# First projection from unnormalised x, the row factor in the activation's scale, and an output projection fed block by block

## The reference

```python
def rmsnorm(x, g):
    xf = x.astype(jnp.float32)
    y = xf * lax.rsqrt(jnp.mean(xf * xf, axis=-1, keepdims=True) + EPS)
    return (y * g.astype(jnp.float32)).astype(x.dtype)

def gmlp_mixer(h, w_in, v_norm_g, w_s, b_s, w_out):
    z = jax.nn.gelu(h @ w_in)
    u, v = jnp.split(z, 2, axis=-1)
    v = rmsnorm(v, v_norm_g)
    w = jnp.where(mask[None], w_s, 0)
    v = v.reshape(B, S // GMLP_BLOCK, GMLP_BLOCK, GMLP_GROUPS, GMLP_GROUP_DIM)
    s = jnp.einsum('gij,bnjgc->bnigc', w, v) + b_s.T[None, None, :, :, None]
    out = u * s.reshape(B, S, GMLP_WIDTH)
    return out @ w_out
...
    h = x
    for l in range(DEPTH):
        if l < N_A_LAYERS:
            h = h + gmlp_mixer(rmsnorm(h, a_norm_g[l]), a_w_in[l], a_v_norm_g[l],
                               a_w_s[l], a_b_s[l], a_w_out[l])
...
        h = h + conv_ffn(rmsnorm(h, f_norm_g[l]), f_w_in[l], f_conv_w[l],
                         f_conv_b[l], f_w_down[l])
```

## Time and profile before

| | us |
|---|---|
| median of 3 runs | 2847.23 |
| lowest and highest | 2845.84, 2847.35 |
| time of the profiled execution | 2847.23 |
| its span in the trace | 2845.2 |
| PE busy in the span | 2670.1 |
| DVE, ACT, POOL busy | 856.2, 565.5, 442.2 |

### The profile page before, as it was taken

The page is one execution under the profiler, slowest core; times in us unless marked ns, Lnnn a source line. Parts: engine busy times, 40 slices in busy tenths (PEclk is TensorE's granted clock), DMA queues, the critical chain, the costliest instruction groups (busy, mean ns, idle before and its releaser), DMA issues. The chain is left out here.

```text
span 2845.2 us, 27418 instructions
## 1 busy us (share of the span) xinstructions
PE 2670.1 (94%) x9989; PEld 1402.6 (49%) x9989; DVE 856.2 (30%) x1933; ACT 565.5 (20%) x1072; POOL 442.2 (16%) x390
## 2 busy tenths in 40 slices
PE   6999999999999999999999989999989999999992
PEld 5644444444656444444444447666745544444440
DVE  2023222102323232221022335556533323222225
ACT  1211111111333211110025542122111111111111
POOL 3004555510000100000121001101110111111110
PEclk8999999999999999999989999999988999999996
DMA  8214555522212222223222110000042699999985
GB/s 172 74 60 133 147 147 147 164 75 57 60 46 60 72 74 74 74 74 84 79 82 74 40 49 25 25 30 16 23 156 89 259 418 416 405 398 400 389 343 213
DMA packets 290831, 407.24 MB, mean 143 GB/s; under 512 B 14258, under 2 KB 253560, under 8 KB 264608
## 3 DMA queue, kind: packets, MB, share of 16 engines
q1 hardware_dynamic: 274048, 366.46, 37.2%
q0 software_dynamic: 16112, 37.19, 4.4%
q10 hardware_dynamic: 560, 2.10, 0.2%
HBM read 396.20 MB, written 30.46 MB: 150 GB/s over the span
## 5 line engine op out<-in xcount | busy, mean ns | idle before, releaser
L925 PE MATMUL bank<-hT,bring 128*128 128x512 f32 x1344 | 582.1, 593 | 0.0
L925 PEld LDWEIGHTS bank<-hT,bring 128*128 128x128 f32 x1344 | 253.8, 190 | 311.9 <-issue 311.9
L864 PE MATMUL bank<-bring 128*128 128x512 f32 x704 | 303.3, 593 | 0.0
L1534 PE MATMUL bank<-bring 128*64 128x512 f32 (+1 forms) x512 | 227.0, 596 | 2.5 <-issue 1.6
L864 PEld LDWEIGHTS bank<-bring 128*128 128x128 f32 x704 | 133.5, 190 | 166.5 <-issue 166.5
L1985 DVE SCALAR_TENSOR_TENSOR ffw<-bank,col,ffw 128x511 f32<-128x511 f32 x88 | 65.9, 749 | 415.0 <-ACT ffw L1633 414.8
L1633 ACT ACTIVATE ffw<-bank,col 128x512 f32<-128x512 f32 x88 | 68.4, 777 | 492.8 <-PE bank L925 470.1
L1970 DVE TENSOR_TENSOR xT<-bank,xT 128x512 f32<-128x512 f32 x32 | 22.1, 691 | 378.2 <-PE bank L864 378.2
L1534 PEld LDWEIGHTS bank<-bring 128*64 128x64 f32 (+1 forms) x512 | 77.8, 157 | 97.7 <-issue 96.5
L663 POOL TENSOR_TENSOR ysq<-ysq 128x512 f32<-128x512 f32 x24 | 30.4, 1268 | 606.7 <-ACT ysq L1605 605.9
L1110 PE MATMUL bank<-hT,bring 128*128 128x512 f32 x256 | 118.7, 611 | 3.6 <-DVE ysq L2142 3.6
(11 more groups left out here) (458 smaller groups left out, 3659.9 us busy)
## 6 DMA issues: line engine op xcount, KB each, us to landing
bring<-f_w_in SPq DMA_DIRECT2D x88, 512.0 KB, 5.3
bring<-exp_w_gate SPq DMA_DIRECT2D x32, 1024.0 KB, 11.0
bring<-exp_w_up SPq DMA_DIRECT2D x32, 1024.0 KB, 19.5
bring<-exp_w_down SPq DMA_DIRECT2D x32, 1024.0 KB, 22.0
two<-ada_w SPq DMA_DIRECT2D x24, 1024.0 KB, 5.3
bring<-f_w_down SPq DMA_DIRECT2D x16, 1408.0 KB, 7.1
two<-exp_w_gate SPq DMA_DIRECT2D x16, 1024.0 KB, 10.1
two<-exp_w_up SPq DMA_DIRECT2D x16, 1024.0 KB, 20.5
```

The costliest lines, as they stand in the source:

```text
L864: mm = pe.matmul(ps[BANKS[stage][n % 4]][:], w[:, k, n % per * P:(n % per + 1) * P], rhs[:, k, :], start=(k == 0), stop=(k == kb - 1))
L925: mm = pe.matmul(ps[2 * j + b][:], w[:, k, b * P:(b + 1) * P], hT[:, k, :], start=(k == 0), stop=(k == KB - 1))
L1534: mm = pe.matmul(ps[3][m * h:m * h + m, :].rearrange("p (m n) -> p m n", m=2), hgT[par][:, k, m * h:m * h + m], w, start=(k == 0), stop=(k ...
```

## The change

- SP issues x, ten rows of gains (tile 0 of `prow`), and then the ring loads. The other 19 parameter rows are issued by ACT, ahead of its first work.
- POOL issues its seven loads behind the constants, and `relR` is the second count of `col_ready`.
- DVE writes `yT`, x times the gain and not normalised, straight from the transposed banks, and gv is computed from `yT`. ACT sums the squares of each token's row from the untransposed x, and the inverse root `row_inv` goes into the takes of gv as the activation's scale.
- `hT`, which gu needs, is made by DVE after unit 0 of gv: PE spreads `row_inv` over 128 partitions into bank 7 by four small products, and DVE multiplies by them. `relR` and the clearing of `wsraw` come behind that on DVE.
- The transposes of the other parameter rows and of `wsraw` move between units 0 and 1 of gu, and the Silu of `c` behind gu.
- go uses banks 4 to 7 and runs its first four output blocks together, k by k. The product of k and n waits only for gated block max(k, n).
- Several semaphores are merged or renamed, and counts of later norms are lowered by one, since the first norm no longer takes part in them.

```diff
--- before.py
+++ after.py
@@ SP: what is left of the parameter loads
-            sp.wait_ge(s("pool_order"), 2)
             for r, ap in ((C_A, a["a_norm_g"][0]), (C_KV, a["kv_norm_g"]), (C_B, a["b_norm_g"][0]),
...
-                row_load(0, r, ap)
-            for l in range(2):
-                row_load(1 + 2 * l, 0, a["f_conv_w"][l, 0:2].rearrange("k c -> (k c)"))
...
+                sp.dma_start(prow[r:r + rows(ap).shape[0], 0, :], rows(ap)).then_inc(s("gains_loaded"), 16)
@@ POOL: seven loads from ahead of the constants to behind them
-            pool.dma_start(favw[:], wcols(a["w_in_2"][0], 2048, 24)).then_inc(s("side_loaded"), 16)
...
-            pool.dma_start(wsraw, a["a_w_s"][0].rearrange("g i j -> i g j")).then_inc(s("ws_loaded"), 16)
...
-            pool.dma_start(relE[:, 0:REL], a["b_rel_bias"][0]).then_inc(s("ws_loaded"), 16)
             porder = Order(pool, s("pool_consts"))
...
             pool.memset(onec[:], 1.0).then_inc(s("consts"), 1)
 
-
-            pool.wait_ge(s("col_ready"), len(PARAM_ROWS) + 2)
+            pool.dma_start(wsraw, a["a_w_s"][0].rearrange("g i j -> i g j")).then_inc(s("ws_loaded"), 16)
...
+            pool.dma_start(relE[:, 0:REL], a["b_rel_bias"][0]).then_inc(s("ws_loaded"), 16)
+            pool.dma_start(favw[:], wcols(a["w_in_2"][0], 2048, 24)).then_inc(s("side_loaded"), 16)
...
+            pool.wait_ge(s("col_ready"), 2)
             pool.dma_start(rel_dram[:, :, 0:RELW], relR[:].unsqueeze(1).to_broadcast([16, P, RELW]))\
                 .then_inc(s("rel_stored"), 16)
@@ PE: the opening
             pe.wait_ge(s("consts"), 3)
+            pe.wait_ge(s("gains_loaded"), 16 * NGAINS)
+            pe.transpose(ps[7][:, 0:P], prow[:, 0, :], ident[:]).then_inc(s("x_turned"), 1)
             pe.wait_ge(s("x_loaded"), 16)
...
-            pe.wait_ge(s("params_loaded"), 16 * NPARAM)
-            for t, rows in enumerate(PARAM_ROWS):
-                wait(pe, s("x_ready"), t + 1)
...
-            pe.wait_ge(s("ws_step"), 3)
-            mean_squares("a")
+
             for u in range(4):
                 ring_ready(pe, "gv", u // 2, u % 2)
                 for t in range(TT):
                     wait(pe, s("gv_taken"), 4 * (u - 2) + t + 1)
+                    if u < 2:
+                        pe.wait_ge(s("x_copied"), 4 * u + t + 1)
                     if u == 1 and t == 3:
 
-                        pe.wait_ge(s("norm_rms_ready"), nth("a"))
+                        pe.wait_ge(s("norm_h_ready"), h_count("a", KB - 1))
                     for k in range(KB):
                         if u == 0 and t == 0:
-                            pe.wait_ge(s("norm_h_ready"), h_count("a", k))
-                        mm = pe.matmul(ps[4 * (u % 2) + t][:, 0:256], hT[:, k, t * P:(t + 1) * P],
+                            pe.wait_ge(s("x_ready"), k + 1)
+                        mm = pe.matmul(ps[4 * (u % 2) + t][:, 0:256], yT[:, k, t * P:(t + 1) * P],
                                        slot(u % 2, 8, 256)[:, k, :], start=(k == 0), stop=(k == KB - 1))
                     mm.then_inc(s("gv_prod"), 1)
-            pe.wait_ge(s("gv_taken"), 16)
+                if u == 0:
+
+                    pe.wait_ge(s("row_inv"), 1)
+                    pe.wait_ge(s("x_copied"), KB)
+                    for t in range(TT):
+                        mm = pe.matmul(ps[7][:, t * P:(t + 1) * P], row_inv[:, t:t + 1].to_broadcast([P, P]), ident[:],
+                                       start=True, stop=True)
+                    mm.then_inc(s("side_prod"), 1)
+            pe.wait_ge(s("gv_taken"), 12)
             for u in range(4):
                 ring_ready(pe, "gu", u // 2, u % 2)
+                if u == 1:
+
+                    pe.wait_ge(s("gv_taken"), 16)
+                    pe.wait_ge(s("params_loaded"), 16 * NPARAM)
+                    for t, rows in enumerate(PARAM_ROWS[1:]):
...
+                    pe.wait_ge(s("ws_step"), 1)
+                    for g in range(8):
+                        tr = pe.transpose(ps[6 + g // 4][:, (g % 4) * P:(g % 4 + 1) * P], wsraw[:, g, :], ident[:])
+                    tr.then_inc(s("ws_step"), 1)
@@ PE: the output projection (its banks are now 4 to 7: "go": (4, 5, 6, 7))
-            pe.wait_ge(s("vn_ready"), TT + 8)
-            linear("go", gT, KB, lambda k: None)
+            for k in range(KB):
+                for n in range(4):
+                    pe.wait_ge(s("vn_ready"), TT + max(k, n) + 1)
+                    linear_step("go", gT, KB, n, k)
+            linear("go", gT, KB, lambda k: None, done=[KB] * 4)
             feed_forward(0)
@@ ACT: the opening
-            for b in range(0, KB, 2):
-                act_e.wait_ge(s("x_turned"), b + 1)
-                act_e.wait_ge(s("x_ready"), b) if b else None
-                nc.scalar.copy(xT[:, b, :], ps[b][:]).then_inc(s("x_ready"), 1)
-            act_e.wait_ge(s("col_ready"), 6)
-            nc.scalar.activation(csil[:], col[:, C_C:C_C + 8], ACT.Silu).then_inc(s("col_ready"), 1)
-            squares("a", "x_ready", KB)
+            act_e.wait_ge(s("pool_order"), 1)
...
+            load_params()
+            act_e.wait_ge(s("x_loaded"), 16)
+            for t in range(TT):
+                row_sq = nc.scalar.activation(sq[:, 2 * t:2 * t + 2, :], x_tok[:, t, :].rearrange("p (a b) -> p a b", a=2), ACT.Square,
+                                              accum_out=ss4[:, t:t + 1])
+            order(row_sq)
+            act_e.wait_ge(s("consts"), 2)
+            nc.scalar.activation(ss4[:, 4:8], ss4[:, 0:4], ACT.Sqrt, scale=1.0 / D, bias=epsc[:])\
+                .then_inc(s("rows_rms"), 1)
+            for b in range(KB):
+                act_e.wait_ge(s("x_ready"), b + 1)
+                nc.scalar.copy(xT[:, b, :], ps[b][:]).then_inc(s("x_copied"), 1)
             act_e.wait_ge(s("consts"), NCONST)
+            act_e.wait_ge(s("row_inv"), 1)
             for u in range(4):
                 for t in range(TT):
                     act_e.wait_ge(s("gv_prod"), 4 * u + t + 1)
                     nc.scalar.activation(vtok[:, t, u * 256:(u + 1) * 256], ps[4 * (u % 2) + t][:, 0:256],
-                                         ACT.Gelu_apprx_tanh).then_inc(s("gv_taken"), 1)
+                                         ACT.Gelu_apprx_tanh, scale=row_inv[:, t:t + 1]).then_inc(s("gv_taken"), 1)
@@ DVE: the opening
-            for b in range(1, KB, 2):
-                dve.wait_ge(s("x_turned"), b + 1)
-                dve.wait_ge(s("x_ready"), b)
-                nc.vector.tensor_copy(xT[:, b, :], ps[b][:]).then_inc(s("x_ready"), 1)
...
+            dve.wait_ge(s("x_turned"), 1)
+            nc.vector.tensor_copy(col[:, 0:P], ps[7][:, 0:P]).then_inc(s("col_ready"), 1)
+            dve.wait_ge(s("col_ready"), 1)
+            for b in range(KB):
+                dve.wait_ge(s("x_turned"), b + 2)
+                nc.vector.tensor_scalar(yT[:, b, :], ps[b][:], col[:, C_A + b:C_A + b + 1], None, ALU.mult).then_inc(s("x_ready"), 1)
+            dve.wait_ge(s("rows_rms"), 1)
+            nc.vector.reciprocal(row_inv[:, 0:4], ss4[:, 4:8]).then_inc(s("row_inv"), 1)
+            dve.wait_ge(s("x_copied"), KB)
+            dve.wait_ge(s("side_prod"), 1)
+            for b in range(KB):
+                nc.vector.scalar_tensor_tensor(out=hT[:, b, :], in0=xT[:, b, :], scalar=col[:, C_A + b:C_A + b + 1], in1=ps[7][:],
+                                               op0=ALU.mult, op1=ALU.mult).then_inc(s("norm_h_ready"), 1)
 
             dve.wait_ge(s("ws_loaded"), 48)
+            nc.vector.memset(wsraw[0:64, :, 64:128], 0.0).then_inc(s("ws_step"), 1)
             order(nc.vector.tensor_copy(relE[:, REL:RELW], relE[:, REL - 1:REL].to_broadcast([16, RELW - REL])))
             nc.vector.tensor_copy(relR[:], relE[:, ::-1]).then_inc(s("col_ready"), 1)
...
-            normalise("a", [(hT, C_A)])
```

More of the change, by code:

```diff
@@ L288, in program @@
             s(n)
[L289 removed]
+        NORMS = ["f0", "att", "f1", "n1", "n2"]
         nth = lambda n: NORMS.index(n) + 1
         def h_count(n, b, out=0):
[L294 to L295 removed]
+            k = 0 if n == "a" else nth(n)
+            return KB * (k + out + (k > nth("att"))) + b + 1
         RAW = {"f0": [(yT, C_F)], "att": [(yT, C_B), (hT, C_KV)], "f1": [(gT, C_F + 8)]}
@@ L836, in mean_squares @@
             def mean_squares(n):
-                if n == "a":
-                    blocks = range(KB)
-                else:
-                    blocks = (0, KB - 1)
-                    pe.wait_ge(s("norm_sum"), 6 * (nth(n) - 1))
-                for b in blocks:
+                pe.wait_ge(s("norm_sum"), 6 * nth(n))
+                if n == "f0":
+                    pe.wait_ge(s("lin_added"), KB)
+                for b in (0, KB - 1):
                     pe.wait_ge(s("norm_sq_ready"), KB * (nth(n) - 1) + b + 1)
@@ new lines, in _, with row_load, load_params @@
+            rows = lambda ap: ap.rearrange("(r c) -> r c", c=P)
+            nload = 0
+            def row_load(tile, r0, flat):
```

(24 more changed lines are left out.)

96 lines of the change are left out of this document (37 added, 59 removed).

## The result

The changed kernel takes 2856.07 us (median of 6 runs, 2854.75 to 2863.04) against 2847.29 for the kernel before in the same jobs. The ratio of the two is 1.0038, with a 95% interval of 1.0026 to 1.0049: slower, inside the forecast range, 6 us under the forecast value.

The account below looks back on a forecast made before the run. PE, 94% busy, was taken as the bound, with the bias table's 46.0 us trip holding gv. 13.0 + 2.2 - 0.5 + 2.7 - 2.5 = +14.9 on 2847.23 gave 2862.1, range 2855 to 2870.

Parts of the forecast that it names:

- Start of gv: Opening: first bank free for gv at 17.5, where the PE path of x and transposes ends; bounds 16 and 20.
- Units 0 and 1 and the start of the trip: gv's unit 0 done at 31.4, unit 1 at 46.2; DVE's copies end at 39.9, POOL stores the bias table at 40.0.
- The trip: Bias table's store and fetch back: slowness its own, still 46.0 us from issue to last write, ending at 86.0.
- the first rival: Store slow only in its old place; at the fetch's rate 19.4 less, 2842.7; chance 0.05 faster, 0.08 within 0.2%.
- Resume and restart: In gv, PE resumes behind the table at 86.6 against 73.59, +13.0, then on the low clock, +2.2.
- gv to gu: Between gv and gu: gu no longer waits for the last take, -0.5.
- Transposes in gu: Inside gu: 13 transposes between products that had no gap, 0.21 each, +2.7.
- go: Output projection: idle 5.98 and low clock 1.8 go; refill gap 3.5 and its clock 1.8 come; sum -2.5.
- the short trip: Bias table's store at the fetch's rate: 15.2 instead of 34.6, total 2842.7; chance 0.05 faster, 0.08 within 0.2%.
- the hidden refill: PE does not stand at block 4 of go; the 3.5 and 1.8 go: 2856.8; chance 0.10.
- the slipping opening: ACT hangs in its 19 loads or unit 0 runs on the low clock: 2.5 and 2.2, up to 2867; chance 0.15.
- with the table out of the way: Rival that the change gains: gv would end some 28 us sooner if the trip fits between 39.9 and 46.2.

Follow-up runs that it names:

- the second profile of this kernel: The changed kernel run once more with no edit, against the kernel before: 2861.47 us, ratio 1.0051.

## Why the prediction was right

*Start of gv.* Forecast 17.5, measured 18.73, inside the bounds, but for a reason that I had not seen. ACT read x from 9.91 on, so x was there. PE did not wait for x but for the ten rows of gains, which now stand ahead of the transposes and land behind x, at 12.39. ACT's 19 loads did not hang.

*Units 0 and 1 and the start of the trip.* The store was forecast for 40.0 and issued at 40.36. Two errors cancel: gv began 1.2 late, while the products on DVE took 5.36 and not 6.0 and the two copies 0.54 and not 1.06.

*The trip.* Forecast 46.0, measured 46.5. The argument that its slowness is its own was right, and the fit of the Trainium skill that the prediction names, which gave the store 9.2 us, held for this store in no run: from 16 partitions it took 34.2 to 35.9 us, 35.1 in the changed kernel, and from 128 still 15.2 to 15.6. In the first rival I wrote that the queue moves the same bytes three times as fast on the way back. By the earlier trace rows it moves two thirds of the bytes, 2.3 times as fast; the rival's price, worked out from the rate, is not touched by it. Another page of the Trainium skill has the rule that fits: "SBUF — State Buffer", section "Door 1: The DMA port swizzle (why `[64,N]` ≈ `[32,N]`)" counts the ports that the partitions reach, at about 27 GB/s each; for partitions 0 to 15 its table has 4 ports of 16 and about 109 GB/s. The trace agrees within a tenth: 1.39 MB in 14 us are 99 GB/s.

*Resume and restart.* Forecast 86.6, measured 87.48, so +13.9 and not +13.0: the store began 0.4 late, the trip took 0.5 more, and a take with a scale read from memory is 0.47 where it was 0.38. The clock was low behind the gap, as forecast: 0.57 from 87.4 to 94.0. Units 2 and 3 took 30.45 up to gu, and 28.34 before: +2.1. That stretch holds two terms of the sum, the restart's +2.2 and the -0.5 of *gv to gu*, so +1.7 was forecast for it.

*Transposes in gu.* gu took 1.4 us longer, for +2.7. I priced them from the opening's transposes, 0.21 each, and inside gu PE runs one in 0.12 (13 from 131.66 to 133.19). Why those of the opening are slower, at a granted clock of 1.00 as well, is not shown; the same 32 took 6.26 us in one profile of the changed kernel and 4.96 in the other.

*go.* 60.2 from the end of the spatial product for 62.5 before: -2.3, for -2.5. The gap was 3.58, for 3.5, and the clock behind it 0.51. The second four blocks took 29.28 where the first four took 27.63, so the clock cost 1.7 here, for 1.8; in the second profile of this kernel they took 30.62, so it cost 3.0.

The sum at the feed-forward layer is +15.1, for +14.9. The steps missed by +0.9, +0.4, -1.3 and +0.2 and cancel in part, so that it agrees to 0.2 is luck, while the mechanism and its order are as forecast. The rivals of the short trip and of the hidden refill fell; gv began 1.2 late, but DVE's faster work made up for most of it, so the slipping opening did not decide. No step had the some 6 us that come back behind the front in a part of the executions. The time lay in the range all the same, but its lower end had been put there for an earlier start, a shorter trip and the clock at the refill, and none of the three came.

What the prediction did not contain is the second wait beneath the first: I wrote that with the table out of the way gv would end 28 us sooner. It would not have. The late ring load stood behind it: without the wait gu began at 92.8, 9 us sooner than in the kernel before, and only with the store from 128 partitions as well at 75.2, 26.7 us sooner.

## What to carry to other kernels

When a change starts a chain earlier, look for what else must be there before its results can be taken, and check whether the same edit moves that later. Here a table that the first product itself doesn't read gated the second half of the first product, through a wait of one engine that reads nothing of it. And before expecting the whole of an idle time back, read from the profile which loads landed inside it: an idle time covers every other lateness of the same length.

A product that sums over blocks as they come should hold only as many weight slots as can be refilled beneath the rest.

## What the runs showed that I had not expected

- A store of 3072 KB takes 34 to 36 us from 16 partitions, in either kind of queue, and 15.2 to 15.6 from 128.
- While such a store runs, a 1 MB load of another queue nearly stops: 27 to 31 us to landing for 5.3 alone. For the first 13 us or so after its issue no packet of it moves. The Trainium skill, "DMA: Bandwidth & Descriptors", section "Queues, rings and completion order", says that each engine takes turns between the queues it has work for, packet by packet. The run without ACT's wait agrees for the time from 62 to 72 us, 217 packets of either queue. It does not show such turns before: 131 packets of the store and none of the load from 48 to 54. With equal numbers of packets the load gets little, as its packets carry 1.0 KB and the store's 4.6.
- The low-clock stretches of the last third fall elsewhere in two executions of the same program, which end 6 us apart. The times of 12 executions show two groups, 3.6 us apart at the nearest, so that medians of six can differ by 5 us without any change.
